# Twelve of the second block's modulation rows on TensorE beside the recurrent unit, and maxima first in VectorE's step

## What is computed

```python
# first block, layer 0 (even) and 1 (odd)
c_act = jax.nn.silu(c)
mod = c_act @ ada_w[l] + ada_b[l]               # 3*1024 values: shift, scale, gate
h = rms_norm(x, norm_g[l]) * (1.0 + scale) + shift
# layer 0: q, k, v, g_a, x_b, g_b = h @ w_in
a_out = diff_attention(q, k, v, ...)             # 4 heads, 2 maps
b_out = bidir_rglru(x_b, ...)                    # gates, a = exp(log_a), scans both ways
y = concat([a_out * silu(g_a), b_out * silu(g_b)]) @ w_out
# layer 1: q, k, v, g = h @ w_in, 16 heads of 64
logits = q @ k^T * scale + bias;  logits = where(col_mask, logits, -inf)
y = (softmax(logits) @ v * silu(g)) @ w_out
x = x + gate * y
# second block: silu(c_2) and silu(c_ctx_2), each times mod_w_2 (2 layers x 3 sub-layers
# x 3 x 1024 columns) plus mod_b_2: the same three vectors for each of six sub-layers
```

## Time and profile before

| | |
|---|---|
| three runs | 2109.81, 2110.72, 2110.95 us (median 2110.72) |
| profiled execution | 2108.35 us, its span 2106.6 us |
| TensorE busy | 1911.6 us, 91% of the span |
| VectorE busy | 1403.9 us, 67% |
| ScalarE busy | 684.1 us, 32% |
| GpSimd busy | 126.5 us, 6% |
| chain that ended last | PE 77%, DVE 14%, ACT 4%, issue 3% |
| its largest line | PE acc L1294, 74% of the span |
| mean granted TensorE clock | 0.956 of full |

### The profile page before, as it was taken

The page is one execution under the profiler, slowest core; times in us unless marked ns, Lnnn a source line. Parts: engine busy times, 40 slices in busy tenths (PEclk is TensorE's granted clock), DMA queues, the critical chain, the costliest instruction groups (busy, mean ns, idle before and its releaser), DMA issues.

```text
span 2106.6 us, 26727 instructions
## 1 busy us (share of the span) xinstructions
PE 1911.6 (91%) x10092; PEld 1624.7 (77%) x10092; DVE 1403.9 (67%) x2091; ACT 684.1 (32%) x910; POOL 126.5 (6%) x78
## 2 busy tenths in 40 slices
PE   2973788879999998999899999989999998988998
PEld 2952777768888887887788888878888887778998
DVE  7877789876666666568766666776666225856554
ACT  2443344432222223332322222132222223344432
POOL 2001200110000010002000000100000010010000
PEclk9975899989999999999899999999999999999999
DMA  9840954424333443334244434433333233224444
GB/s 376 321 155 20 235 196 176 155 90 150 149 149 131 165 158 135 147 140 171 90 149 149 144 129 167 173 114 135 145 149 121 96 102 121 90 76 142 161 162 158
DMA packets 75737, 315.77 MB, mean 150 GB/s; under 512 B 19060, under 2 KB 22904, under 8 KB 56344
## 3 DMA queue, kind: packets, MB, share of 16 engines
q1 hardware_dynamic: 75136, 314.15, 41.9%
q10 hardware_dynamic: 536, 0.79, 0.1%
HBM read 313.86 MB, written 1.06 MB: 149 GB/s over the span
## 4 chain that ended last, share of the span: by engine, by line
PE 77%; DVE 14%; ACT 4%; issue 3%; DMA 1%; POOL 1%; SPq 0%; DVEq 0%; ACTq 0%
PE acc L1294 74%; DVE Wl L809 3%; ACT Wh L525 2%; PE psN L1294 2%; DVE tmp L796 1%; DVE psGT L841 1%; DVE psGT L838 1%; DVE psGT L844 1%; DVE XT L796 1%; DMA afirst<-in_ada_w 1%; PE psN L1356 1%; DVE small L966 0%; PE psGT L1294 0%; DVE psGT L1057 0%; PE psT L1400 0%
## 5 line engine op out<-in xcount | busy, mean ns | idle before, releaser
L1294 PE MATMUL acc<-Hh,Wh 128*128 128x512 f32 (+1 forms) x2320 | 806.9, 348 | 55.4 <-DVE Hl L796 23.4
L1294 PE MATMUL acc<-Hl,Wh 128*128 128x512 f32 (+1 forms) x2320 | 798.9, 344 | 0.0
L1294 PE MATMUL acc<-Hh,Wl 128*128 128x512 f32 (+1 forms) x2320 | 798.2, 344 | 0.0
L809 DVE TENSOR_TENSOR Wl<-raw,Wh 128x2048 fp32r<-128x2048 f32 (+1 forms) x214 | 449.6, 2101 | 284.1 <-ACT Wh L525 283.9
L1294 PEld LDWEIGHTS acc<-Hh,Wh 128*128 128x128 f32 x2320 | 447.3, 193 | 118.8 <-issue 64.3
L525 ACT ACTIVATE Wh<-raw 128x2048 fp32r<-128x2048 f32 (+1 forms) x214 | 374.3, 1749 | 353.2 <-PE acc L1294 335.7
L1294 PEld LDWEIGHTS acc<-Hl,Wh 128*128 128x128 f32 x2320 | 447.4, 193 | 50.9 <-issue 0.7
L1294 PEld LDWEIGHTS acc<-Hh,Wl 128*128 128x128 f32 x2320 | 446.7, 193 | 50.2
L1294 PE MATMUL acc<-hidh,Wh 128*128 128x512 f32 (+1 forms) x704 | 258.6, 367 | 0.9 <-DVE Wl L809 0.9
L1294 PE MATMUL acc<-hidl,Wh 128*128 128x512 f32 (+1 forms) x704 | 258.3, 367 | 0.0
L1294 PE MATMUL acc<-hidh,Wl 128*128 128x512 f32 (+1 forms) x704 | 258.2, 367 | 0.0
(11 more groups left out here) (222 smaller groups left out, 1201.5 us busy)
## 6 DMA issues: line engine op xcount, KB each, us to landing
raw<-in_ffn_up SPq DMA_DIRECT2D x88, 1024.0 KB, 4.8
graw<-in_mod_w SPq DMA_DIRECT2D x144, 512.0 KB, 5.5
raw<-in_ffn_down SPq DMA_DIRECT2D x64, 704.0 KB, 4.1
graw<-in_ada_w SPq DMA_DIRECT2D x32, 512.0 KB, 5.8
raw<-in_odd_in SPq DMA_DIRECT2D x16, 1024.0 KB, 4.8
raw<-in_even_in SPq DMA_DIRECT2D x12, 1024.0 KB, 6.3
raw<-in_conv_in SPq DMA_DIRECT2D x12, 1024.0 KB, 4.8
afirst<-in_ada_w SPq DMA_DIRECT2D x8, 1024.0 KB, 13.2
```

Of the source, the lines that this page charges most:

```text
L809: nc.vector.tensor_tensor(Wl[:, half, 0:f], raw[:, slot, 0:f], Wh[:, half, 0:f].bitcast(f32), ALU.subtract)\
L1294: return nc.tensor.matmul(out, lhsT, rhs, start=start, stop=stop)
```

## The change

- STAGES: odd_in goes from one row per tile to none, gqa_out from none to one per tile. Sixteen rows leave odd_in, four come to gqa_out, twelve are left.
- These twelve, the first of mod_w, get numbers between even_in and even_out and are computed on TensorE after the sums of squares. First the two condition vectors are turned onto partitions (16 matmuls with one moving column into psG, a copy with the factor 0.5 to cT). Then for each row: eight 128x128 transposes into a pair of PSUM banks (weight_turned), two copies of 128x512 to SBUF by ScalarE (weight_copies), and eight matmuls with the turned row as weights and two moving columns (weight_mixed). Two rows are turned ahead of the spreads that VectorE waits for. ScalarE copies two rows ahead of its square root, eight between that and its tanh, two after it.
- VectorE adds the bias to all twelve at once (take_turned) between the recurrent unit and even_out's first residual step, and waits there for the last product.
- SyncE issues the twelve loads after even_in's.
- In odd_in VectorE's step begins with the maxima, then comes the weight split; the masks of the eight pairs of heads are added in tiles 0 to 4 (MASK_AT), with the wait for the bias table moved from tile 3 to tile 0.
- Later rows are taken earlier or later by some tiles; at_row replaces takes in the waits for them.

```diff
...
     ("even_out", 4, 16, 0, LAT, 2, "dve"),
-    ("odd_in", 16, 16, 0, LAT, 1, "act"),
+    ("odd_in", 16, 16, 0, LAT, 0, "act"),
     ("odd_out", 4, 16, LAT, LAT, 1, "dve"),
...
     ("gqa_q", 4, 16, 0, LAT, 1, "act"),
-    ("gqa_out", 4, 16, 0, LAT, 0, "dve"),
+    ("gqa_out", 4, 16, 0, LAT, 1, "dve"),
     ("ffn3_up", FC, 16, 0, LAT, 0, "dve"),
...
 FIRST = 2 * KC
+TURNED0 = FIRST + 24
+TURNED = 12
+MOD0 = 2 * ADA_TILES + TURNED
+
+
+def weight_row(g):
+
+    if g < TURNED0:
+        return "ada_w", g
+    if g < TURNED0 + TURNED:
+        return "mod_w", g - TURNED0
+    if g < MOD0:
+        return "ada_w", g - TURNED
+    return "mod_w", g - 2 * ADA_TILES
...
         rounds += tiles if gemv else 0
+        if name == "even_in":
+            g += TURNED
+            rounds += 1
         drained[by] += tiles
...
+        turnedW = view("turnedW", 24 * KB, [P, 2, D])
+
...
         c_tanh = sem("c_tanh")
+        ct_ps, ct_cp, w_copied, w_mixed = sem("ct_ps"), sem("ct_cp"), sem("w_copied"), sem("w_mixed")
...
         gres = [small[:, 192 + 8 * b:200 + 8 * b] for b in range(2)]
+        cT = small[:, 208:224]
         sp4 = small[:, 240:248]
...
         TAKE_AT = {6: (0,), 8: (1,), 14: (2, 3), 15: (4, 5), 16: (6,), 17: (7,)}
+        MASK_AT = {0: (0, 1), 1: (2, 3), 2: (4, 5), 3: (6,), 4: (7,)}
         GATE_DONE = {4: 0, 14: 1, 15: 2, 16: 3}
...
                             continue
-                        if s.name == "even_in" or isinstance(g, int) and g < 2 * ADA_TILES:
-                            load_g("ada_w", g, g, slot, g if isinstance(g, int) else None)
+                        if isinstance(g, int):
+                            load_g(weight_row(g)[0], g, weight_row(g)[1], slot, g)
+                        elif s.name == "even_in":
+                            load_g("ada_w", g, g, slot, None)
                         else:
...
                 tiles(sp, s, PER, LEAD, step, head={"even_in": 1, "odd_in": 4, "conv_in": 3}.get(s.name, 0))
+                if s.name == "even_in":
+                    for g in range(TURNED0 + LEADG, TURNED0 + TURNED + LEADG):
+                        load_g(weight_row(g)[0], g, weight_row(g)[1], g % GRAW, g)
             sp.wait_ge(drained["dve"], S["ffn3_down"].drained1)
...
             nc.scalar.activation(sga, ev[:, 12:16, :], ACT.Tanh, scale=0.5).then_inc(ev_th, 1)
+            act.wait_ge(ct_ps, 1)
+            nc.scalar.activation(cT, psG[:, 0:16], ACT.Copy, scale=0.5).then_inc(ct_cp, 1)
+
+            def weight_copies(r):
+                act.wait_ge(g_done, TURNED0 + r + 1)
+                if r >= 2:
+                    act.wait_ge(w_mixed, r - 1)
+                for j in range(2):
+                    ins = nc.scalar.activation(turnedW[:, r % 2, j * 512:(j + 1) * 512], (acc[1], psT)[r % 2][j][:, 0:512], ACT.Copy)
+                ins.then_inc(w_copied, 1)
+
+            for r in range(2):
+                weight_copies(r)
             act.wait_ge(lru_m2, 1)
             nc.scalar.activation(tT[:, :, :], tT[:, :, :], ACT.Sqrt).then_inc(lru_mult, 1)
+            for r in range(2, TURNED - 2):
+                weight_copies(r)
             act.wait_ge(lru_hs, 1)
             nc.scalar.activation(aT[:, 0:4, :], ev[:, 20:24, :], ACT.Tanh, scale=0.5).then_inc(ev_th, 1)
+            for r in range(TURNED - 2, TURNED):
+                weight_copies(r)
             splits(S["even_out"])
...
+            def g_low(g):
+
+                return not isinstance(g, int) or g < TURNED0
+
+            def take_turned():
+
+                dve.wait_ge(w_mixed, TURNED)
+                n = 2 * TURNED
+                nc.vector.tensor_tensor(mod[:, 0, 0:TURNED, :].rearrange("p m b -> p (m b)"), psG[:, 16:16 + n], V("mod_b", 0, n),
+                                        ALU.add).then_inc(g_taken, 1)
+                dve.wait_ge(g_taken, S["even_out"].round0)
+
...
                 if first:
-                    c, at_, b = g, ada[:, :, :].rearrange("p l m -> p (l m)"), COL["ada_b"]
+                    c, at_, b = g if g_low(g) else g - TURNED, ada[:, :, :].rearrange("p l m -> p (l m)"), COL["ada_b"]
                 else:
...
                                                op1=ALU.mult, accum_out=gres[u % 2][:, 2 * q:2 * q + 1]).then_inc(g_half, 1)
-                dve.wait_ge(g_half, g - 2 * ADA_TILES + 1)
+                dve.wait_ge(g_half, g - MOD0 + 1)
                 nc.vector.scalar_tensor_tensor(out=junk[:, :], in0=graw[:, slot, :], scalar=0.5, in1=cb[:, 1, :], op0=ALU.mult,
...
+            def at_row(name, m):
+
+                return next(takes(g) for g in range(NG) if weight_row(g) == (name, m)) if name == "ada_w" or m >= TURNED else 0
+
...
-                dve.wait_ge(g_taken, takes(l * ADA_TILES + 2 * KC - 1))
+                dve.wait_ge(g_taken, at_row("ada_w", l * ADA_TILES + 2 * KC - 1))
                 link(stt(ada[:, l, KC:2 * KC], ada[:, l, KC:2 * KC], 1.0, V("norm_g", l * KC, KC), ALU.add, ALU.mult))
...
-                dve.wait_ge(g_taken, takes((2 + l * 3 + sub) * ADA_TILES + 2 * KC - 1))
+                dve.wait_ge(g_taken, at_row("mod_w", (l * 3 + sub) * ADA_TILES + 2 * KC - 1))
                 sc = mod[:, l, (sub * 3 + 1) * KC:(sub * 3 + 2) * KC, :].rearrange("p m b -> p (m b)")
...
-                dve.wait_ge(g_taken, takes((3 + l * 3 + sub) * ADA_TILES - 1))
+                dve.wait_ge(g_taken, at_row("mod_w", (l * 3 + sub + 1) * ADA_TILES - 1))
                 ga = mod[:, l, (sub * 3 + 2) * KC:(sub * 3 + 3) * KC, :].rearrange("p m b -> p (m b)")
...
                 two_parts(4 + c, gates[:, 1, c, :])
+            take_turned()
             residual(S["even_out"])
...
                 now = UNITS_AT.get(t, ())
-                split(s.n0 + t + 1)
-                for u in now:
-                    if u == 0:
-                        dve.wait_ge(ld_nab, 12 * 16)
-                    if u % 2 == 0:
-                        masked(u // 2)
                 if now:
...
                     maxes(na, u)
-                modulation_of(s, t, t % PER, t // PER, najunk)
+                split(s.n0 + t + 1)
+                if t == 0:
+                    dve.wait_ge(ld_nab, 12 * 16)
+                for g in MASK_AT.get(t, ()):
+                    masked(g)
                 for u in now:
...
             ins.then_inc(ot_ss, 1)
+            for k in range(KC):
+                for b in range(2):
+                    ins = mm(psG[:, 2 * k + b:2 * k + b + 1], cb[:, b, k * P:(k + 1) * P], ident[:, 0:1], True, True)
+            ins.then_inc(ct_ps, 1)
+
+            def weight_turned(r):
+                g = TURNED0 + r
+                pe.wait_ge(g_loaded[g % GRAW], 16 * ((g - FIRST) // GRAW + 1))
+                if r >= 2:
+                    pe.wait_ge(w_copied, r - 1)
+                for k in range(KC):
+                    ins = nc.tensor.transpose((acc[1], psT)[r % 2][k // 4][:, (k % 4) * P:(k % 4 + 1) * P],
+                                              graw[:, g % GRAW, k * P:(k + 1) * P], ident[:, :])
+                ins.then_inc(g_done, 1)
+
+            def weight_mixed(r):
+                pe.wait_ge(w_copied, r + 1)
+                if r == 0:
+                    pe.wait_ge(ct_cp, 1)
+                for k in range(KC):
+                    ins = mm(psG[:, 16 + 2 * r:18 + 2 * r], turnedW[:, r % 2, k * P:(k + 1) * P], cT[:, 2 * k:2 * k + 2],
+                             k == 0, k == KC - 1)
+                ins.then_inc(w_mixed, 1)
+
+            weight_turned(0)
+            weight_turned(1)
             pe.wait_ge(ot_rstd, 1)
...
             ins.then_inc(ot_spread, 1)
+            for r in range(TURNED):
+                weight_mixed(r)
+                if r + 2 < TURNED:
+                    weight_turned(r + 2)
             linear(S["even_out"], together=True)
```

## The result

The changed kernel takes 2123.89 us (median of four, 2122.57 to 2126.40) against 2110.31 us for the kernel before (four, 2109.81 to 2110.95): a ratio of 1.0066, 95% interval 1.0048 to 1.0083. It is **13.6 us slower**; the forecast was 29.0 us slower. The span of the profiled execution is 2122.2 us, 15.6 more than before.

A forecast was written before the change was run, and what follows sets the result against it. TensorE's acc matmuls were taken to carry about three quarters of the chain, with other bounds in short stretches. +46.6 - 23.3 + 5.7 = +29.0 on 2108.35 gave 2137.3; the median's 2.37 more gave 2139.7 us, 8-in-10 range 2127 to 2149.

The forecast's parts named there:

- if the clock is up in the new work: Sign that the prediction is wrong: TensorE's clock above 0.50 in the twelve rows' work beside the recurrent unit.
- even_out did not start before 240: Other sign that the prediction is wrong: even_out starting before 240 us; its first matmul was forecast near 251.
- Part 1: Twelve rows on TensorE beside the recurrent unit, at 1.2 GHz throughout: even_out starts at 251.3, not 204.7, +46.6 us.
- the bound of +40: Lower bound for the twelve rows' cost, if 24 transposes in a row raise the clock for a few us.
- the second rival: 24 transposes in a row raise the clock and the small matmuls hold it: about -5, 2105.5 us; 4%.
- the first rival: Clock rises beside the recurrent unit, up by about 176.8; kernel faster by 11.2, 2099.5 us; 9%.
- What I costed at nothing: Ahead of even_out: row loads, ScalarE's copies and late tanh, VectorE's added wait, all taken as hidden under TensorE's work.
- Part 2: odd_in without its sixteen rows, maxima first: 14.8 idle, 3.1 clock and 5.4 tail, 23.3 us won; bounds 16 and 26.
- the tail: From tile 15's end in odd_in to the weight split of odd_out's second tile: 14.7 us to 9.3, 5.4 won.
- The step in the prediction: One odd_in step: VectorE splits, masks, forms logits, finishes the maximum at 291.3; exponentials wait, TensorE idles 3.53 us.
- Part 3: Four rows added in gqa_out on VectorE: the last residual ends at 1900.2, +5.7 us; bounds 3 and 7.
- The lower bound of 3: gqa_out's four rows cost 3 us if there is no contention with GpSimd, 2.6 us a row.

The follow-up runs named there:

- run 2: Against the changed kernel: the twelve rows come from memory with the input dimension on the partitions, so no transposes or copies, two-column multiplications kept; 2106.16 us, ratio 0.9981.
- run 5: Against the changed kernel: seven of the eight two-column multiplications of each row left out, all transposes and copies kept; 2092.23 us (one run).
- run 1: Against the changed kernel: TensorE's and ScalarE's share of the twelve rows left out, their loads still made; 2085.36 us, ratio 0.9883.
- run 6: Against a kernel with laid-out rows streamed and the condition as weights: the condition laid out too, its 16 turning matmuls gone; 2092.82 us, ratio 0.9919.
- run 9: Against the kernel before: only VectorE's order in odd_in changed (maxima first, masks in tiles 0 to 4), all sixteen rows kept; 2091.58 us, ratio 0.9918.
- run 10: Against the changed kernel: VectorE's old order in odd_in (split and masks first, then maxima), the rows still gone; 2146.36 us, ratio 1.0175.
- the best version: Against run 6: two rows multiplied ahead of the spreads, and ScalarE's tanh ahead of the later copies; 2087.83 us, ratio 0.9900.

## Why the prediction was wrong in size

The sign was right, and in the main the mechanism: a strand of small matmuls, at the half clock for all but 3.4 us, that TensorE works off while even_out waits. The forecast was 15.8 us too high, and the measured time lies under the range's lower end of 2127. By its own sign "if the clock is up in the new work" it was wrong for those 3.4 us; even_out did not start before 240.

- **Part 1, the term that failed: +46.6 forecast, +37.7 measured.** The start slipped by 1.0 us, and the condition, two turned rows and spreads came 1.0 us cheaper, so up to 188.8 us the forecast holds to the tenth. Behind it stand 53.6 us where I had 62.5, 8.9 less. *First,* I priced a row in an unbroken strand by the durations of groups that had stood alone, each after an idle TensorE: 3.57 for 16 records and 1.97 for a turn. In the strand the timeline shows 3.41 and 1.95, and these overlap at their ends; the chain counts them once, 3.21 and 1.81, and a row repeats every 5.0 us and not 5.54. Twelve times 0.36 and ten times 0.16 are 5.9 us. Even the bound of +40 was built on the shown durations. *Second,* the clock rose at 188.7 for 3.4 us: 1.44 and 0.82 us saved on two multiplications and 0.88 on a turn, 3.1 us. That stood in my bounds (24 transposes that "raise the clock for a few us") and in the second rival, whose first half came true; but the two-column multiplications didn't hold it.
- **The clock in the rest** was as forecast, and for the reason given: the earlier trace rows had shown busy one-column matmuls at 0.50, and run 2 shows 39 us of the two-column kind at 0.50. A slip in the first rival changes nothing here: 2.9 us after 172.16 is 175.1, not 176.8, which would have ended its strand 1 us earlier. The hint of the Trainium skill, "TensorE: Matmul & The Clock Gate", Part 4, that the full clock doesn't engage for transposes, isn't borne out: it was full through run 5's transposes.
- **What I costed at nothing was hidden** up to even_out's start: the loads (run 1), the tanh behind the copies and VectorE's wait (the chain is TensorE's alone). Whether the 0.7 us that even_out itself took longer come from VectorE's wait, no run tells. All this holds only under a strand this long; with a short one VectorE waited 5.6 us for the tanh (run 6).
- **Part 2: -23.3 forecast, -25.0 measured**, with no idle time left ahead of the value products and 6.9 us won in the tail against 5.4. The sum was right, but it didn't say which half of the edit earns it, and when I had to say so ahead of runs 9 and 10, I gave it to the rows. The step in the prediction had the right answer: the maximum is late because the split stands ahead of it.
- **Part 3: +5.7 forecast, +3.4 measured.** I took 2.32 and 2.11 us a multiply-sum beside GpSimd from odd_out. Here they took 1.75 to 1.77 and up to 1.59, and the first of the four rows 1.23. The lower bound of 3 was the better value.
- **The sum:** the three terms are off by 8.9 + 1.7 + 2.3 = 12.9 us. Besides, even_out cost 0.7 and the stretch behind gqa_out 0.4, and 1.6 came back between odd_out and gqa_out, which makes 13.4, from the forecast +29.0 to the +15.6 of the spans. The other 2.4 up to 15.8 are that the medians stand 13.6 apart, and that the kernel before had a median of 2110.31 here, not 2110.72.

## What to carry to other kernels

Where a two-column operand meets a 128 x 128 one, make the two columns the weights and stream the large one: here that cut the strand from 40.7 to 25.9 us and kept the clock up. Before moving work off an engine that seems full, look at what stands at the head of its queue: changing the order of one step gave 18.4 of the 22.1 us that the best version won, and without it removing 39 us of work gave 3. Moved work is free only if it is ready when the hole opens. And the duration of a group that stood alone isn't its pace in a row: the distance between the starts of equal groups that follow one another gives that.

## What the hardware showed that I had not expected

**Transposes are followed by the full clock.** In the changed kernel and in run 5 it rose within 6 us of the first of them, from 0.50 to 1.00, with only one-column matmuls before them (from 173.1 and 172.2 us on); in run 2, with the same one-column matmuls and spreads (these are eight transposes, too) but two-column multiplications in place of the sixteen others, it didn't rise before even_out. Two windows of run 5, whose transposes begin at 182.5 us:

```profile
186.50:187.00 0.50, 0.50 (x5) 0.50 (x4) 0.00 (x0) 0.50 (x2) 0.00 (x0) 0.50 0.98 401
187.00:187.50 0.50, 0.50 (x6) 0.50 (x6) 0.00 (x0) 0.48 (x2) 0.00 (x0) 0.94 0.59 172
```

**How long the clock stayed up varied with the same instructions.** In run 10, whose strand is that of the change, it was full from 186.0 to 196.3 us, and not from 188.7 to 192.1. One group of multiplications ahead of the fall and one behind it, in TensorE's timeline:

```profile
192.43 1.84 PE L1354 MATMUL psGT<-small,turnedW 128*128 128x2 f32 x16
...
199.00 3.41 PE L1354 MATMUL psGT<-small,turnedW 128*128 128x2 f32 x16
```

even_out began 6.5 us earlier there (235.9 us), all but 0.2 us of it by that. What decides it I haven't tested. Run 10's five times spread over 6.2 us, the widest of the study; whether that is the same effect from one execution to the next, no trace here shows.
